# The first block's attention with a stage of slack between scores and transposes, and a third score buffer

## The reference, cut to what matters

```python
def first_block(x, c, ...):
    for l in range(2):                        # DEPTH
        h = rms_norm(x, g_pre_mix[l]) * (1.0 + sc_m) + sh_m
        y = token_mixer(h, w_in[l], g_moba_out[l], g_dsa_out[l], w_out[l], cos, sin)
        x = x + gt_m * rms_norm(y, g_post_mix[l])
        h = rms_norm(x, g_pre_ffn[l]) * (1.0 + sc_f) + sh_f
        x = x + gt_f * rms_norm(conv_glu_ffn(h, ...), g_post_ffn[l])

def token_mixer(h, w_in, ...):
    # 8 heads of causal attention (seq 256 is one block of MoBA), 8 heads over the 64 best keys of an index score
    o_moba = moba_attention(mq, mk, mv)
    o_dsa = dsa_attention(dq, dk, dv, qi, ki, wi)
    return jnp.concatenate([rms_norm(o_moba, g_moba_out), rms_norm(o_dsa, g_dsa_out)], axis=-1) @ w_out
# attention, per head: softmax(mask(q @ k.T / 8)) @ v
```

## Time and profile before

| | |
|---|---|
| median of 3 runs | 3739.69 us (3738.66 to 3740.0) |
| the profiled execution | 3734.57 us, span 3733.3 us |
| mean granted clock of PE | 0.923 |
| busy: PE | 2993.4 us, 80% of the span |
| busy: DVE | 2457.5 us, 66% |
| busy: ACT | 773.4 us, 21% |
| busy: POOL | 929.9 us, 25% |
| DMA | 1102 MB, mean 295 GB/s |
| layer 0's attention | from 493.2 us (first mask) to 602.5 us (end of o7) |
| layer 1's attention | from 1213.0 us to 1273.7 us |

### The profile page before, as it was taken

One profiled execution on the slowest core, in us unless ns is written; L12 is line 12 of the kernel. 1 busy time (PEld: TensorE's weight loads), 2 busy tenths in 40 slices (PEclk: granted clock), 3 DMA queues, 4 the chain that ended last, 5 costly groups with the idle time before them and its releaser, 6 DMA issues. The chain is left out here.

```text
span 3733.3 us, 28494 instructions
## 1 busy us (share of the span) xinstructions
PE 2993.4 (80%) x8761; PEld 1565.5 (42%) x8761; DVE 2457.5 (66%) x5372; ACT 773.4 (21%) x1865; POOL 929.9 (25%) x842
## 2 busy tenths in 40 slices
PE   6899887799897789969777777777798787778776
PEld 1354465566333458435445223322244462223222
DVE  2225367798576778746658999666533459996665
ACT  1102133233222533124511111000112211110000
POOL 0000001222222133223312434433200014344342
PEclk7899887899998899979888999999988889999999
DMA  6555335899797579958747999999742159999998
GB/s 227 197 183 179 131 104 188 311 355 361 294 367 275 198 310 417 417 204 343 260 166 278 389 390 389 421 422 421 305 174 98 62 213 389 392 382 412 422 422 345
DMA packets 205546, 1102.17 MB, mean 295 GB/s; under 512 B 23796, under 2 KB 24128, under 8 KB 107088
## 3 DMA queue, kind: packets, MB, share of 16 engines
q0 software_dynamic: 114512, 818.87, 55.2%
q1 hardware_dynamic: 90256, 280.91, 20.7%
q10 hardware_dynamic: 624, 0.57, 0.0%
HBM read 1099.18 MB, written 1.05 MB: 295 GB/s over the span
## 5 line engine op out<-in xcount | busy, mean ns | idle before, releaser
L2106 PE MATMUL PS<-AR 128*128 128x512 f32 x2456 | 1198.8, 633 | 397.3 <-DVE AR L2148 343.3
L2205 POOL DMA_INDIRECT AR<-in_uv,AR x768 | 854.9, 1113 | 1691.5 <-PE PS L2106 1124.0
L2153 DVE CUSTOM_DVE_ANT_0 AR<-AR 128x1024 f32<-128x1024 f32 x768 | 935.5, 1221 | 322.2 <-DMA AR<-in_uv,AR 321.6
L2106 PEld LDWEIGHTS PS<-AR 128*128 128x128 f32 x2456 | 467.3, 199 | 1079.3 <-DVE AR L2148 536.1
L750 PE MATMUL PS<-AR 128*128 128x512 f32 (+4 forms) x1176 | 510.9, 588 | 36.0 <-ACT AR L2337 15.7
L2118 ACT ACTIVATE AR<-AR 128x2 f32<-128x2 f32 x384 | 78.1, 203 | 1530.0 <-DVE AR L2153 1513.3
L750 PEld LDWEIGHTS PS<-AR 128*128 128x128 f32 x1176 | 225.5, 206 | 294.6 <-issue 250.3
L1051 PE MATMUL PS<-AR 128*128 128x256 f32 x1408 | 317.3, 384 | 4.0 <-DMA AR<-in_w_up_lin 2.3
L350 DVE SCALAR_TENSOR_TENSOR AR<-AR,CC 128x512 f32<-128x512 f32 x280 | 210.4, 752 | 164.1 <-DMA AR<-in_w_ada 100.6
L1051 PEld LDWEIGHTS PS<-AR 128*128 128x128 f32 x1408 | 267.9, 192 | 64.5 <-issue 19.4
L2025 PE MATMUL PS<-AR 128*128 128x256 f32 x768 | 189.6, 410 | 20.7 <-DMA AR<-in_peer_w_q 17.6
(11 more groups left out here) (226 smaller groups left out, 2514.4 us busy)
## 6 DMA issues: line engine op xcount, KB each, us to landing
AR<-in_w_mod SPq DMA_DIRECT2D x96, 512.0 KB, 4.4
AR<-in_w_ada SPq DMA_DIRECT2D x160, 256.0 KB, 6.1
AR<-in_w_in SPq DMA_DIRECT2D x56, 512.0 KB, 4.5
AR<-in_peer_w_q SPq DMA_DIRECT2D x48, 512.0 KB, 3.3
AR<-in_w_up_act SPq DMA_DIRECT2D x44, 512.0 KB, 9.7
AR<-in_w_up_lin SPq DMA_DIRECT2D x44, 512.0 KB, 8.9
AR<-in_w_down SPq DMA_DIRECT2D x44, 512.0 KB, 10.6
AR<-in_even_w_in SPq DMA_DIRECT2D x24, 512.0 KB, 5.2
```

The source lines that it names most:

```text
L2106: ins = pe.eng.matmul(acc[i][hh], e.dg(x), e.buf(x)[:, 1024 + 512 * hh:1536 + 512 * hh], start=(x == e.on[False][i][0]), stop=(x == e.on[F ...
L2153: v.eng.tensor_tensor_reduce(e.buf(x)[:, 0:1024], e.buf(x)[:, 0:1024], norm2(e).H[e.tiles[x // 128]], 1.0, 0.0, ALU.mult, ALU.add, DT[x // ...
L2205: g.eng.indirect_dma_start(e.buf(x), None, D["uv"][e.l], bass.IndirectOffsetOnAxis(ap=idx_at(x // 16, x % 16, 1), axis=0)).then_inc(*land. ...
```

## The change

In the first block's attention a part that does nothing is put between s1 and s2. The transposes of a unit's weights, and all that follows for it, come one step later: in step i the scores are those of unit i, the transposes those of unit i - 2 and av is that of unit i - 3. On ACT the exp stays in step i and its evictions move to the unit i - 2. Each attention now has 11 steps, so that SP and POOL, which do nothing in them, yield 11 times too. As a unit's exps now live one step longer, there is a third score buffer, in columns 3072 to 4095 of the scratch tile T, and the mask write waits for the transposes of three units before. The two buffers for turned weights (`PT1`) and the PSUM banks are as they were. No arithmetic is added or left out.

```diff
--- before.py
+++ after.py
@@ -899,7 +899,7 @@
         PR = view(BIG, 0, 2, 3656)
         SCO, MSK = [pr(t, 3072, 512).rearrange("p (a b) -> p a b", b=256) for t in range(2)]
         R1 = view(T, 2048, 8, 256)
-        SB1 = [pr(0, a, 1024).rearrange("p (a b) -> p a b", b=256) for a in (0, 1536)]
+        SB1 = [b.rearrange("p (a b) -> p a b", b=256) for b in (pr(0, 0, 1024), pr(0, 1536, 1024), T[:, 3072:4096])]
         PT1 = [pr(1, a, 1024).rearrange("p (a b) -> p a b", b=128) for a in (0, 1536)]
         O1 = view(T, 0, 2, 1024)
         GT = view(BIG, 0, 22, 256)
@@ -1007,7 +1007,7 @@
                     pe.wait_ge(("p", l, u))
                     for i in range(4):
                         ins = pe.eng.transpose(bk[:, i * 128:(i + 1) * 128],
-                                               SB1[u % 2][:, i, kt * 128:(kt + 1) * 128], ident)
+                                               SB1[u % 3][:, i, kt * 128:(kt + 1) * 128], ident)
                     ins.then_inc(*pe.done("mm", "pt", l, u, kt))
 
             def s3(u):
@@ -1023,7 +1023,7 @@
                                             PR[:, kt, v0 + h * 64:v0 + h * 64 + 64], start=(kt == 0), stop=(kt == t))
                 ins.then_inc(*pe.done("mm", "av", l, u))
 
-            for _ in stages(8, s1, s2, s3):
+            for _ in stages(8, s1, nothing, s2, s3):
                 yield ATT[l]
             yield 1.0
             seen = {}
@@ -1092,7 +1092,7 @@
             sp.flush()
             yield 1.0
             yield 1.0
-            for _ in range(10):
+            for _ in range(11):
                 yield ATT[l]
             yield 1.0
             for _ in lin(sp, 8, (0, 1024), [0, 1], nothing):
@@ -1221,7 +1221,7 @@
                 kw = 128 * (t + 1)
                 a.wait_ge(a.last, ("nm", l, u))
                 for i in range(4):
-                    a.eng.activation(SB1[u % 2][:, i, 0:kw], SB1[u % 2][:, i, 0:kw], ACT.Exp,
+                    a.eng.activation(SB1[u % 3][:, i, 0:kw], SB1[u % 3][:, i, 0:kw], ACT.Exp,
                                      bias=sm(4, "anm", u % 4)[:, i:i + 1],
                                      accum_out=sm(4, "asu", u % 4)[:, i:i + 1]).then_inc(
                         *a.done(*(("p", l, u) if i == 3 else ())))
@@ -1234,7 +1234,7 @@
                                  psum("pt", l, u, kt).rearrange("p (a b) -> p a b", b=128), ("mm", "pt", l, u, kt),
                                  ("mm", "av", l, u - 2) if u >= 2 else None).then_inc(*a.done("ev", "pt", l, u, kt))
 
-            for _ in stages(8, s1, s2, nothing):
+            for _ in stages(8, s1, nothing, s2, nothing):
                 yield ATT[l]
             for t in range(2):
                 rstd_act(a, (("of", t), l), [O1[:, t, k * 512:k * 512 + 512] for k in range(2)], 512,
@@ -1377,11 +1377,11 @@
                         for _ in st:
                             pass
                 mask = cst("cm")[:, t * 256:t * 256 + kw] if kind == 0 else MSK[:, t, 0:kw]
-                sbuf = SB1[u % 2]
+                sbuf = SB1[u % 3]
                 for i in range(2):
                     src = psum("sc", l, u, i).rearrange("p (a b) -> p a b", b=256)[:, :, 0:kw]
                     v.wait_ge(v.last, ("mm", "sc", l, u),
-                              [("mm", "pt", l, u - 2, kt) for kt in range(units1[u - 2][1] + 1)] if u >= 2 else None)
+                              [("mm", "pt", l, u - 3, kt) for kt in range(units1[u - 3][1] + 1)] if u >= 3 else None)
                     v.eng.scalar_tensor_tensor(out=sbuf[:, i:i + 3:2, 0:kw], in0=src, scalar=0.125,
                                                in1=mask.unsqueeze(1).to_broadcast([128, 2, kw]), op0=ALU.mult,
                                                op1=ALU.add).then_inc(*v.done("ev", "sc", l, u, i))
```

## The result

The changed kernel takes 3721.1 us (median of 5 runs, 3712.65 to 3723.68) against 3739.7 us before: a ratio of 0.9947, 95% interval 0.9932 to 0.9962, or 18.6 us less. The profiled execution took 3718.16 us.

What follows compares the result with a forecast made beforehand. In layer 0's attention DVE and PE were taken as about equally full, taking turns; PE bounds the feed-forward and layer 1's output projection. Terms 6.6 - 3.9 - 3.5 = -0.8 us gave 3738.9 us, no change, range 3727 to 3750.

Steps and rivals of the forecast that it cites:

- term e: Output projection of layer 1: two of four expert sums stand elsewhere, -3.5 us, ends 0 and -10.
- Term d: Layer 1's attention: DVE's waits on PE mostly go, -5.1, one added dot costs 1.2; -3.9 us, ends -7.0 and 0.
- a: Steps 0 to 9 of layer 0's attention: half of PE's 4.8 us gained, -2.5 us, ends 0 and -8.0.
- b: Layer 0, first expert dot to last product (o7): added background stands ahead of it, +11.0 us, ends 8 and 13.
- c: Layer 0, from o7 to the norm's output (L1427): dots 1 to 3 already done, 16.2 us instead of 18.1, -1.9.
- all go but the last av's 1.9: Layer 1's attention: of DVE's 7.0 us of waits on PE only the last av's 1.9 stay, -5.1 us.
- f: Feed-forward: rows 3.6 off the place their engine numbers were set for, taken as 0, ends -3.5 and +3.5 us.
- the 4 us that the prediction named as a sign of being wrong: Feed-forward part: the forecast is wrong if its length changes by over 4 us.
- the waits were the loss: Rival, faster: one unit of slack frees PE and DVE, which hand work back and forth; -14.7 us, 3725; chance 0.27.
- -10 for rows paced by their arrival: Tail, the output projection of layer 1: 3.6 rows leave a stretch paced by row arrivals, -10 us.
- The rival of the drain: Slower: layer 0's extra step puts dots and a cold expert sum before av7; +9.6 us in all, 3749; chance 0.23.
- nothing is given back: Layer 0's steps 0 to 9 gain 0, layer 1 -1, the tail 0, so +9.1 us in layer 0's drain stays.

Runs made afterwards that it cites:

- e1: The changed kernel with the eleventh attention step yielding a share of 0 in both layers; ratio 0.9987 to the kernel before.
- e2: The kernel before, old order and two score buffers, with one empty step behind each layer's attention yielding 1.2 and 0.5 shares; ratio 0.9947.
- e14: The kernel before with 0.17 shares more in each of the first ten steps of the latents' mixer; ratio 1.0004.
- e4: The kernel before with the new stages and third score buffer in layer 1 only; ratio 1.0025.

## Why the prediction was wrong

In short, the step that put the time outside the range is term e: of the latents' mixer only the output projection was costed, at -3.5 us, and the mixer became 19.9 us shorter. Term d had the wrong sign, which hid part of this, and the input projection, -11.6, was in no term.

**a, b, c. Layer 0.** The lengths came out right: -2.3, +10.2 and -1.5 against -2.5, +11.0 and -1.9, together +6.4 where +6.6 was forecast. For a this was luck. It took half of 4.8 us by which PE was to run shorter; PE's idle time grew by 3.6 us instead, and DVE's work ahead of the dot fell by 1.4 us, which are charged again in b, and its waits by 0.7. In b the path was right (the dot, ACT's load and diagonal, row 0's sum, av7), with the av 1.75 us quicker than taken, at the length of the full clock. (The terms of b as listed add to 13.5, not 13.4; nothing hangs on it.) That the new order, not the buffer, shortens these steps was right (104.2 us in the change, 103.6 in e1, 105.9 in e2), though it carries nothing in sum: e1, without the added share, still takes 128.4 us to the norm against 127.0.

**d. Layer 1, forecast -3.9, measured +6.7 to the norm's output.** The step that failed is "all go but the last av's 1.9": DVE's waits for PE were 9.5 us where 7.0 stood. e1 shows the order alone at +2.9 (72.2 against 69.3), and e2 the shares alone at +8.0 (77.3). The share brought two dots and not one. The two effects don't add up, and what each wait costs here was not followed.

**e. Forecast -3.5, ends 0 and -10; measured -19.9.** This is the step that failed and put the result outside the range. What it calls the output projection of layer 1 (1852 to 1889) is the last part of the latents' mixer, into which the background comes four rows further on (60 dots left before, 56 after; 3.6 had been taken). I read these 37 us and took the two sums that leave them, which came true; the other 250 us of the mixer were not costed, and the lower end was again a price by row. What the runs show in its place: the mixer has two lengths, 268 to 278 or 285 to 290 us, set by how far the background is at its start (short at 1.7 and 3.6 shares, long at 0, 0.5, 1.2 and 2.4); in the change 9 of its 19.9 us come at the seam, and by PE 13 of them are less busy time, at a granted clock of 0.91 in place of 0.86, and 7 less idle time.

**f. Feed-forward, forecast 0 with ends of 3.5.** Layer 0's was -5.9, layer 1's -1.2. The first lies outside the ends and past the 4 us that the prediction named as a sign of being wrong; but with nothing ahead in layer 0 this part takes 338.5 to 343.9 us and with 1.2 shares in the attention 334.5 to 338.9, so some 4 us of it are the effect.

**Not named at all:** layer 1's input projection, -11.6. It was in no term of the sum, without a reason; the change edits nothing there.

The rival "the waits were the loss" came nearest, 3725, mostly for the wrong reason: DVE's waits went from 8.0 to 7.3 us in layer 0's steps and from 7.0 to 9.5 in layer 1. Its -10 for rows paced by their arrival has something to it: DVE's waits for rows in the mixer fell by 10.8 us. The rival of the drain had its +9.1 confirmed (+8.7) and its "nothing is given back" refuted.

What stays open: why 56 and 52 rows in the mixer are good and 54, 57, 58 and 60 are not. A step of four fits 56 and 52 and not 60. How much of the mixer's gain is the position of the rows and how much their number is not separated by e14. Why the input projection is shorter with 1.2 shares and less so with 1.7 was not tested. And e4's loss of 0.25% was not followed.

## What to carry to other kernels

In a program that weaves a background into a foreground by shares, any step added to the foreground moves everything behind it. Cost the whole rest of the program for that, above all the stretches that the edit doesn't touch, and test an edit with its added shares set to 0 before crediting it. A small load in a queue behind a row gather, or a root behind a gelu, can be the end of a chain that starts on other engines. Try several positions as a parameter, since the gain is not monotonic in them.

## What was not expected of the hardware

The same 750 or so matmuls of the mixer cost PE 230.3 us at a granted clock of 0.86 and 217.4 at 0.91. In the change 7 us less of idle time went with 13 us less of busy time, in e2 9 with 9: if the clock rose because the waits were gone, which no run isolates, a wait taken away paid two to three times. What speaks for it stands above: row 0's sum behind an idle time of 5.53 us took 3.51 us, and four matmuls of the same shape in the output projection took 1.88.

The load of a gain row that POOL issued at 1626.91, between two row gathers, let L363 start only at 1638.87, 12 us later. It is 512 KB once repeated over the partitions, and not a slow one among its like: in the trace before, POOL's loads of gain rows landed 3.6 to 20.6 us after their issue.
